# Latent attention of the second token stream in the first stream's PSUM banks: a hybrid attention, mLSTM and expert step on one core

## What is computed

```python
mod = (silu(cvec) @ ada_w[l] + ada_b[l])          # 1024 -> 6144, for both streams
sh1, sc1, g1, sh2, sc2, g2 = split(mod, 6)
xn = rms_norm(x, norm1_g[l]) * (1 + sc1) + sh1
aq, ak, av, bq, bk, bv, bo, bg, cq, ckv, ckr = split(xn @ w_in[l])   # 1024 -> 2096
oa = attention(norm(aq), norm(ak), av, sink)      # group A: 6 heads, 2 kv heads; stream 1 also sees 128 cached keys
ob = mlstm(bq, bk, bv, bo, bg, state)             # group B: 4 heads, both directions
oc = latent_attention(cq, ckv, ckr, w_uq, w_ukv)  # group C: 6 heads of 96; stream 1 also sees 128 cached tokens
x = x + g1 * (concat(oa, ob, oc) @ w_out[l])
x = x + g2 * ffn(rms_norm(x, norm2_g[l]) * (1 + sc2) + sh2)   # layer 0 dense SwiGLU, layer 1 top 2 of 8 experts
```

## Time and profile before

| | |
|---|---|
| median of 3 runs | 1622.07 us (1617.94 to 1623.02) |
| span of the profiled execution | 1619.0 us (the profile gives no other time of it) |
| TensorE busy | 1530.0 us, 95% |
| VectorE / ScalarE busy | 1164.3 us, 72% / 916.9 us, 57% |
| loads by the DMA | 523.26 MB, mean 323 GB/s |

### The profile page before, as it was taken

One profiled execution on the slowest core, in us unless ns is written; L12 is line 12 of the kernel. 1 busy time (PEld: TensorE's weight loads), 2 busy tenths in 40 slices (PEclk: granted clock), 3 DMA queues, 4 the chain that ended last, 5 costly groups with the idle time before them and its releaser, 6 DMA issues.

```text
span 1619.0 us, 19723 instructions
## 1 busy us (share of the span) xinstructions
PE 1530.0 (95%) x7058; PEld 1173.1 (72%) x7058; DVE 1164.3 (72%) x1222; ACT 916.9 (57%) x791; POOL 70.7 (4%) x113
## 2 busy tenths in 40 slices
PE   6888879999998788999999999999999999999998
PEld 3455448888656545788888888888888888888886
DVE  1364555444445355789888888888889888889998
ACT  1213234443232322677877877777877877777774
POOL 1610000000001000100000000000000000000200
PEclk9999999999997697899999999999999999999999
DMA  9969978865786275799999999999999999999994
GB/s 360 324 195 415 365 258 269 268 200 186 257 276 194 91 268 201 285 383 369 388 373 384 385 375 375 383 376 373 385 377 378 379 380 379 377 381 365 390 403 157
DMA packets 192825, 523.26 MB, mean 323 GB/s; under 512 B 10880, under 2 KB 71456, under 8 KB 187656
## 3 DMA queue, kind: packets, MB, share of 16 engines
q1 hardware_dynamic: 167440, 493.39, 82.7%
q0 software_dynamic: 7024, 18.63, 3.5%
q10 hardware_dynamic: 18312, 10.60, 2.2%
HBM read 505.50 MB, written 17.08 MB: 323 GB/s over the span
## 4 chain that ended last, share of the span: by engine, by line
PE 81%; DVE 9%; ACT 5%; issue 3%; DMA 3%; SPq 0%; DVEq 0%; ACTq 0%
PE PS L605 21%; PE PS L607 20%; PE PS L606 20%; PE PS L720 5%; PE PS L611 4%; DVE parts L2049 2%; PE PS L935 2%; DMA ring<-in_ada_w 2%; PE PS L686 1%; PE PS L734 1%; ACT parts L1442 1%; PE PS L750 1%; ACT arena L1279 1%; DMA ring<-in_w_in 1%; PE PS L625 1%
## 5 line engine op out<-in xcount | busy, mean ns | idle before, releaser
L2049 DVE TENSOR_TENSOR parts<-ring,parts 128x2048 fp32r<-128x2048 f32 x336 | 765.5, 2290 | 103.7 <-ACT parts L1442 101.1
L1442 ACT ACTIVATE parts<-ring 128x2048 fp32r<-128x2048 f32 x336 | 644.2, 1920 | 218.4 <-PE PS L607 218.4
L605 PE MATMUL PS<-parts 128*128 128x512 f32 x1608 | 634.4, 395 | 8.4 <-DVE parts L1688 4.1
L607 PE MATMUL PS<-parts 128*128 128x512 f32 x1608 | 627.9, 390 | 0.0
L606 PE MATMUL PS<-parts 128*128 128x512 f32 x1608 | 627.4, 390 | 0.0
L605 PEld LDWEIGHTS PS<-parts 128*128 128x128 f32 x1608 | 302.4, 188 | 76.5 <-DVE parts L2049 9.3
L607 PEld LDWEIGHTS PS<-parts 128*128 128x128 f32 x1608 | 302.3, 188 | 64.5
L606 PEld LDWEIGHTS PS<-parts 128*128 128x128 f32 x1608 | 302.6, 188 | 61.8 <-issue 0.2
L1602 DVE TENSOR_TENSOR parts<-ring,parts 128x2048 fp32r<-128x2048 f32 x33 | 75.5, 2289 | 52.4 <-PE PS L607 49.6
L720 PE MATMUL PS<-ring,xnT 128*128 128x420 f32 (+1 forms) x240 | 91.6, 532 | 0.0
L1220 ACT ACTIVATE parts<-ring 128x2048 fp32r<-128x2048 f32 x33 | 63.0, 1915 | 29.8 <-PE PS L607 29.8
(11 more groups left out here) (314 smaller groups left out, 939.4 us busy)
## 6 DMA issues: line engine op xcount, KB each, us to landing
ring<-in_moe_w SPq DMA_DIRECT2D x336, 1024.0 KB, 6.9
ring<-in_ada_w SPq DMA_DIRECT2D x40, 1024.0 KB, 9.6
ring<-in_w_in SPq DMA_DIRECT2D x32, 840.0 KB, 11.6
ring<-in_ffn_w SPq DMA_DIRECT2D x44, 512.0 KB, 5.4
ring<-in_w_out SPq DMA_DIRECT2D x16, 1024.0 KB, 8.0
ring<-in_ffn_w SPq DMA_DIRECT2D x11, 1024.0 KB, 4.8
expert_rows<-zeros ACTq DMA_DIRECT2D x17, 512.0 KB, 4.9
ring<-in_ada_w SPq DMA_DIRECT2D x16, 512.0 KB, 11.4
```

Of the source, the lines that this page charges most:

```text
L605: mm(out, s_hi, m_hi, start=start, stop=False)
L607: return mm(out, s_lo, m_hi, start=False, stop=stop)
L1442: A(w_hi(j), slot(n), ACT.Copy).then_inc(hi_ready, 1)
L2049: TT(w_lo(j, 3), slot(W0 + j), w_hi(j).bitcast(f32), ALU.subtract).then_inc(split_done, 1)
```

## The change

Stream 1's group C runs in banks 0 to 3 and in stream 0's scratch, that is in the places of C0 and not of A1 and B1. Its first step waits for C0's result (`oC`) and no longer for B1's (`num_read`). In turn stream 0's output projection (transposes in banks 4 and 5, result in 4 and 5) and the modulation pieces behind the first `A1` (banks 6 and 7) move to the banks in which B1 runs, and wait for B1's `num_read`. ScalarE's C1.3 has a new wait on the stores of the mLSTM's state, which lie in that scratch. The list is rewritten for both layers: C1's steps stand among A1's and B1's, and the `a` and `o0` tokens behind B1.5.

```diff
-PHASE_1 = {0: """
-A0 i1 A0 i1 A0 i1 A0 B0 i1 B0 i1 n1 B0 i1 i1 B0 B0 t0 i1 C0 t0 i1 C0 t0 i1 C0 a a a a a C0 g1 a C0 a a C0 a C0
-""", 1: """
-A0 i1 A0 i1 A0 i1 A0 B0 i1 B0 i1 n1 B0 i1 B0 B0 t0 i1 C0 t0 t0 i1 C0 i1 C0 i1 A1 A1 C0 g1 C0 l1 c1 A1 C0 A1 C0
-""}
-PHASE_2 = {0: """
-A1 l1 a A1 a c1 a a A1 a A1 B1 a B1 a B1 a o0 o0 B1 B1 a C1 t1 a C1 t1 t1 a C1 o0 a o0 a a C1 a C1 a a o0 C1 r0 r0 a C1
-""", 1: """
-a B1 a B1 a B1 o0 o0 B1 B1 a C1 t1 C1 t1 t1 a C1 o0 a o0 C1 a C1 a o0 C1 r0 r0 a C1
-""}
+ORDER = {0: """
+i1 A0 i1 A0 i1 A0 A0 B0 i1 B0 i1 n1 B0 i1 B0 i1 B0 t0 i1 C0 t0 i1 t0 C0 C0 i1 a a a C0 a a C0 g1 a a a C0 a
+c1 l1 A1 C0 A1 C1 C1 A1 C1 A1 B1 C1 B1 C1 B1 B1 C1 B1 a t1 t1 a t1 o0 a a C1 a o0 a o0 a o0 a a o0 r0 a a r0
+a a a a a a a
+""", 1: """
+A0 i1 A0 i1 i1 A0 i1 A0 B0 B0 n1 B0 B0 i1 B0 i1 t0 i1 C0 t0 t0 i1 g1 C0 i1 C0 i1 l1 A1 c1 C0 A1 C0 A1 C0 A1
+B1 C0 B1 C1 B1 B1 C1 B1 t1 C1 a a t1 a o0 a a a t1 a C1 o0 C1 o0 o0 C1 o0 r0 r0 a C1 a
+""}
...
+        def lane(X, s):
+            return 0 if X == "C" else s
...
         def oT(s):
-            return R(s, 4096 if s else QKT, 1024)
+            return R(1, 4096 if s else QK, 1024)
+
+        def o_banks(s):
+            return (6, 7) if s else (4, 5)
...
             l = 0 if g < early_of[0] else 1
-            return (4, 5) if g < g_after_1[l] else (2, 3)
+            return (4, 5) if g < g_after_1[l] else (6, 7)
...
                     if g == g_after_1[g >= early_of[0]]:
-                        wait("oC", 2 * (g >= early_of[0]) + 1)
+                        wait("num_read", 2 * (g >= early_of[0]) + 2)
...
             def group_C(l, s):
                 u = 2 * l + s
-                b0 = 4 * s
+                b0 = 0
                 wait("cn_ready", u + 1)
-                wait("num_read", u + 1)
                 if s == 0:
+                    wait("num_read", u + 1)
                     wait("state_copied", l + 1)
+                else:
+                    wait("oC", u)
...
             def out_proj(l, s):
                 wait("oC", 2 * l + s + 1)
+                if s == 0:
+                    wait("num_read", 2 * l + 2)
+                b0 = 0 if s else 4
...
                 if s == 1:
+                    act.wait_ge(state_out[l], 16 * 3)
                     summed(act, first["ukv", l, 1])
```

More of the change, by code:

```diff
@@ L31 @@
 PER_EXPERT = 3 * sum(PIECES)
-PHASE_1 = {0: """
-A0 i1 A0 i1 A0 i1 A0 B0 i1 B0 i1 n1 B0 i1 i1 B0 B0 t0 i1 C0 t0 i1 C0 t0 i1 C0 a a a a a C0 g1 a C0 a a C0 a C0
+ORDER = {0: """
+i1 A0 i1 A0 i1 A0 A0 B0 i1 B0 i1 n1 B0 i1 B0 i1 B0 t0 i1 C0 t0 i1 t0 C0 C0 i1 a a a C0 a a C0 g1 a a a C0 a
+c1 l1 A1 C0 A1 C1 C1 A1 C1 A1 B1 C1 B1 C1 B1 B1 C1 B1 a t1 t1 a t1 o0 a a C1 a o0 a o0 a o0 a a o0 r0 a a r0
+a a a a a a a
 """, 1: """
-A0 i1 A0 i1 A0 i1 A0 B0 i1 B0 i1 n1 B0 i1 B0 B0 t0 i1 C0 t0 t0 i1 C0 i1 C0 i1 A1 A1 C0 g1 C0 l1 c1 A1 C0 A1 C0
-"""}
-PHASE_2 = {0: """
-A1 l1 a A1 a c1 a a A1 a A1 B1 a B1 a B1 a o0 o0 B1 B1 a C1 t1 a C1 t1 t1 a C1 o0 a o0 a a C1 a C1 a a o0 C1 r0 r0 a C1
-""", 1: """
-a B1 a B1 a B1 o0 o0 B1 B1 a C1 t1 C1 t1 t1 a C1 o0 a o0 C1 a C1 a o0 C1 r0 r0 a C1
-"""}
-PLAN = [(PHASE_1[l] + PHASE_2[l]).split() for l in range(2)]
+A0 i1 A0 i1 i1 A0 i1 A0 B0 B0 n1 B0 B0 i1 B0 i1 t0 i1 C0 t0 t0 i1 g1 C0 i1 C0 i1 l1 A1 c1 C0 A1 C0 A1 C0 A1
+B1 C0 B1 C1 B1 B1 C1 B1 t1 C1 a a t1 a o0 a a a t1 a C1 o0 C1 o0 o0 C1 o0 r0 r0 a C1 a
+"""}
+PLAN = [ORDER[l].split() for l in range(2)]
 CONST = {}
@@ L727, in scores_softmax_out @@
                 u = 2 * l + s
-                b0 = 4 * s
+                sc = lane(X, s)
+                b0 = 4 * sc
                 for hi in range(6):
@@ L904, in group_C @@
                     wait("TC2_a", l + 1)
-                qkT = R(s, QKT, nh * 128, 96)
+                qkT = R(0, QKT, nh * 128, 96)
                 def qT(hi):
@@ L1287, in softmax @@
                 n = 512 * n_kt
-                A(R(s, QK, n), banks(4 * s, n), ACT.Copy).then_inc(Q["PT" + X + "_a"], 1)
+                A(R(sc, QK, n), banks(4 * sc, n), ACT.Copy).then_inc(Q["PT" + X + "_a"], 1)
                 yield
@@ L1340, in group_C @@
                     wait("C_mm", l + 1)
-                heads = R(s, QK, 18 * 96).rearrange("p (h d) -> p h d", h=18)
+                heads = R(0, QK, 18 * 96).rearrange("p (h d) -> p h d", h=18)
                 def halves(b, n):
                     return PS[:, b:b + 2, 0:n]
-                A(R(s, QK, 576).rearrange("p (a n) -> p a n", a=2), halves(b0, 288), ACT.Copy)
+                A(R(0, QK, 576).rearrange("p (a n) -> p a n", a=2), halves(b0, 288), ACT.Copy)
                 def kv(set_):
@@ L1718, in softmax @@
                 if X == "A":
-                    link(TT(c_(s, "ls"), c_(s, "ls"), c_(s, "es"), ALU.add))
-                link(v.reciprocal(c_(s, "rinv"), c_(s, "ls")))
+                    link(TT(c_(sc, "ls"), c_(sc, "ls"), c_(sc, "es"), ALU.add))
+                link(v.reciprocal(c_(sc, "rinv"), c_(sc, "ls")))
                 wait("PT" + X, u + 1)
                 n, all_ = 512 * n_kt, 768 * n_kt
-                v.tensor_copy(R(s, QK + n, all_ - n), banks(4 * s, all_)[:, n:all_]).then_inc(Q["PT" + X + "_d"], 1)
+                v.tensor_copy(R(sc, QK + n, all_ - n), banks(4 * sc, all_)[:, n:all_]).then_inc(Q["PT" + X + "_d"], 1)
                 yield
@@ L1899, in group_C @@
                 nh = 12 + 6 * s
-                qk = R(s, QK, nh * 96).rearrange("p (h d) -> p h d", h=nh)
-                sq = R(s, SQ, nh * 96).rearrange("p (h d) -> p h d", h=nh)
-                link(RED(c_(s, "tmp", nh), sq, AX.X, ALU.add))
-                link(TS(c_(s, "var", nh), c_(s, "tmp", nh), 1.0 / C_QK, EPS, ALU.mult, ALU.add))
-                r = rsqrt(s, nh)
+                qk = R(0, QK, nh * 96).rearrange("p (h d) -> p h d", h=nh)
+                sq = R(0, SQ, nh * 96).rearrange("p (h d) -> p h d", h=nh)
+                link(RED(c_(0, "tmp", nh), sq, AX.X, ALU.add))
+                link(TS(c_(0, "var", nh), c_(0, "tmp", nh), 1.0 / C_QK, EPS, ALU.mult, ALU.add))
+                r = rsqrt(0, nh)
                 last = TT(qk[:, 6:nh, :], qk[:, 6:nh, :], r[:, 6:nh].unsqueeze(2).broadcast_to([128, nh - 6, C_QK]), ALU.mult)
@@ L1911, in group_C @@
                     last = rope(tail, tail, K("cosC"), K("sinC"), 12, 16,
-                                [R(s, SQ + 192 * i, 192).rearrange("p (h d) -> p h d", h=12) for i in range(4)])
+                                [R(0, SQ + 192 * i, 192).rearrange("p (h d) -> p h d", h=12) for i in range(4)])
                 last.then_inc(Q["qkC_ready"], 1)
-                TS(c_(s, "sq"), r[:, 0:6], C_QK ** -0.5, None, ALU.mult)
+                TS(c_(0, "sq"), r[:, 0:6], C_QK ** -0.5, None, ALU.mult)
                 yield
```

65 lines of the change are left out of this document (33 added, 32 removed).

## The result

| | before | changed |
|---|---|---|
| median of 19 runs each | 1622.07 us (1617.91 to 1624.92) | 1626.17 us (1624.01 to 1632.16) |
| ratio | | 1.0034, interval 1.0024 to 1.0043 |
| span of the profiled execution | 1619.0 us | 1630.4 us (its run, 1631.97, is one of the slowest of the 19) |

Slower, as forecast, and inside the range; but 4.1 us and not 14. The profiled execution of the changed kernel lies 5.8 us above its median, so I compare stretches inside the two traces and leave the spans alone. A1.1 is the first step of stream 1's group A, B1.5 the last of its group B, and out1 the first transposes of its output projection behind the list; a stand is time in which TensorE is idle. First the stretches of the changed kernel, which answer to the earlier trace rows: length, busy us (instructions) of TensorE, its weight loads, VectorE, ScalarE and GpSimd, then TensorE clock, DMA share, GB/s.

The account below looks back on a forecast made before the run. The prediction took layer 0's mixer as bound by its loads and layer 1's by stream 1's chain A1, B1, C1. It summed 1622.07 + 20 (layer 0) - 5.6 (layer 1) = 1636 us, range 1625 to 1650.

Parts of the forecast that it names:

- +20: Layer 0: the FFN starts later because its loads arrive later, and nothing behind it gives this back; booked +20 us.
- -5.6: Layer 1: out1 starts 3.6 us earlier and 2 us come from the clock being up at its first products.
- bound of -14: Layer 1's best end: full clock from B1 on, about 8 us more gain than the booked -5.6.
- C1.1 and C1.2 come in with some 6 at half clock: Layer 1, way to B1.5: these two steps of C1, now ahead of it, add some 6 us.
- 4 and 9.6 us less: Layer 1, way to B1.5: two `a` pieces (4 us) and o0.2 with its stand (3.66 + 5.95) leave it.
- "faster" rival: Stream 1's two chains really run side by side: T 36 us after A1.1, layer 1 wins 14, 1613 us; 7%.
- T: Layer 0: the point at which a.10, the first `a` piece waiting for B1's read, may start; forecast 185.5 us.
- T to the FFN: Layer 0: loads and TensorE run side by side, the DMA's path is longer; FFN at T + 60.9, 246.4 us.
- the estimate from that ceiling: Layer 0: at 435 GB/s the 19.9 MB take 45.8 us, both paths are equal, and the layer loses 15.
- TensorE's path: Layer 0: by TensorE's own work and stands, out1 would start at T + 38.5 and the FFN at T + 54.8.
- the hole: Layer 0: a gap in the DMA's rate from about 155 to 186 us, the load ring being full until T.
- The much slower one: Rival: half clock in layer 0's whole stretch, T = 194.8, layer 0 +30 and layer 1 -2, 1650 us; 14%.

Follow-up runs that it names:

- the old head: Layer 0 as before, layer 1 as in the changed kernel, but layer 1's list up to the first A1 as before: 1605.91 us, again 1607.51 us.
- the new head: Layer 1 as in the changed kernel, with its rewritten list up to the first A1, layer 0 as before: 1602.32 us, again 1601.75 us.

## Why the prediction was right in sign and wrong in size

**The sum.** Forecast +20 and -5.6, together 14; measured +24.2 and -20.0, together 4. The way layer 0 loses and the sign of each layer were right. Layer 1's gain lay outside its own bound of -14, and the prediction had named a gain over 14 as what would make it wrong. That the time still fell inside the range, 1 us above its lower end, is luck: layer 0's loss, 4.2 us larger than booked, made up for a part of it.

**Layer 1, A1.1 to out1: the step that failed.** The prediction said "C1.1 and C1.2 come in with some 6 at half clock" and took the durations of a stretch with the clock at 0.62. Its sum is not clean here: 4 and 9.6 us less and 6 more put B1.5 38.7 us behind A1.1, its "about 5.6 earlier" 40.7. It came at 30.7, with the clock at 0.83, where it was 0.67 before. Two runs show which term was mis-sized. With C1 wholly behind B1 the way to B1.5 takes 32.7 us, and with C1.1 and C1.2 in it 30.2: the term booked at +6 measured -2.5, since the two steps run in stands of A1 and B1. And with the clock at 0.62 the same steps (the old head's first profile) took 40.0 us, about the forecast; at 0.83 and 0.84 they took 30.2 and 32.3. So the links were counted rightly, and the size was off by the clock and by the stands. The prediction carried over the granted clock of a stretch whose work the change itself rearranges. I had seen the bound ("full clock from B1 on, about 8 more") and put it at the end of the range and not in its middle. Up to C1.4 the forecast was 10.4 us too long (56.9 against 46.5), 8 to 10 of them ahead of B1.5. The rest of the 14.4 us is 1.3 from C1.4 to out1, 0.9 behind out1 (2.9 against 2), and 1.8 at the head, +3.0 against +4.8 by the distance from the FFN's first product (294.9 against 291.9).

**Where that gain came from.** C1 behind B1 leaves 5 us of the 20. The other 15 come from C1's first steps standing among A1's and B1's. For both together, the stands up to out1 fall from 20.9 in the kernel before to 11.0 us and the busy time from 73.2 to 63.0 us at an equal count of instructions (383 and 382). The prediction's "faster" rival had this mechanism for both layers; the Trainium skill, page "Perfetto Trace Analysis", section Optimization Strategy, says that interleaving regimes can gain. Layer 1 agrees with it, 20 us; layer 0 with the same interleaving lost 24.

**Layer 0, T.** Forecast A1.1 + 52.2, measured 53.5 (55.7, 53.0 and 55.9 in other profiles of this list). Right by its steps in the changed kernel's own profile: C1.3 to C1.4 took 12.63 us (forecast 12.6), B1.3 to B1.5 8.3 (8.5), the read 5.2 (4.7); C1.2 to C1.3 took 7.3 (5.25) and C1.4 to the scores 6.2 (4.5), both with pieces at half clock in them. The 3 us booked for the clock were a little short: the four profiles lie 3.7 to 6.6 us above the sum at full clock, 49.3. T came at 186.6 to 193.4 in the four profiles, inside the 182 to 195 named.

**Layer 0, T to the FFN.** Forecast 60.9, measured 63.5, and by nearly the steps given: the FFN's first load landed at T + 55.4 (forecast 52.7), and from the start of its split to the FFN's first product it took 8.1 (8.2). The 19.9 MB were reckoned at 389 GB/s, and the stretch from T to the FFN had 370. The Trainium skill, page "DMA: Bandwidth & Descriptors", section Bandwidth, puts the ceiling at 435 GB/s; the fastest 20 us behind T (210 to 230) had 422, but the whole way stayed well below, so the estimate from that ceiling, -15 for layer 0, was the worse one. TensorE's path, forecast at T + 54.8, was not refuted: the run with the a loads halved has 53.6 without its waits for loads. Relieving the loads alone gives back 6 of the 24 us. Two thirds of the loss lie ahead of T, as forecast; the lists that let B1 go ahead of C1.3, and `a` pieces into the hole, brought 12 and 16 of the 24 us back.

**Costed at nothing.** ScalarE's new wait for the state's stores cost nothing that a row shows: in C1.3 it waits 0.80 us, and for TensorE. That the head of layer 0's list shifts steps by under 0.5 us can't be told from the runs: A1.1 was forecast at 133.3 and came at 133.7, 134.1, 134.2 and 139.9 in four profiles of the list, so the scatter between executions is larger than the term.

**The rivals.** Of the faster one (7%), the gain of layer 1 came and exceeded its 14; its T at A1.1 + 36 did not. The much slower one (14%) is borne out in part: layer 0 from A1.1 to T had a clock of 0.75, below the 0.91 of before, and T lay at A1.1 + 53 to 56 instead of its 61. Of what was to show it, T, the `a` pieces' and the split's waits for loads came as named, and the hole too, from 165 to 195 instead of 155 to 186; the FFN came at 256.9 and not at 246; on the FFN's base C1.4 of layer 1 came 25.5 us earlier and not 13, and out1 17.1 and not 4; and layer 1 won more than 14, which the prediction had named as what would make it wrong.

**Best version.** Layer 1's change with layer 0 as before: 1602.3 and, again, 1601.75 us, 1.2 to 1.3% under before.

## What to carry to other kernels

Run each stage's part of a change alone before judging the whole: here a change that measured +0.3% was -1.2% in one layer and +1.5% in the other. Here the interleaving paid where the stage had stands to fill (layer 1, DMA share 0.59) and cost where the pieces that it pushed back were what kept the loads going (layer 0, DMA share 1.02). When a list is reordered, ask anew for TensorE's clock in the stretch: durations from a half-clock stretch hold only if its stands and its mix of products stay; and move a piece into a stand only after looking at what each of its operands waits for on the other engines.

## What the runs showed of the hardware

TensorE's granted clock in one stretch of one program is not fixed. The list with the old head ran A1.1 to B1.5 at 0.62 in one execution and at 0.84 in another, 40.0 and 32.3 us, and its eight times fall into 1603 to 1605 and 1608 to 1612. With the new head, whose wait at the start of the stretch is 1 us shorter (0.42 against 1.35 to 1.57), none of eight runs took over 1604; that the wait is the cause is not shown. It is so elsewhere too: in the same two executions out1 to the FFN in layer 0 took 16.3 us at 1.00 in the one and 19.2 us at 0.82 in the other. The first of these is the execution that had 0.62 in layer 1, so the two stretches do not fall together. The Trainium skill, page "TensorE: Matmul & The Clock Gate", section "What's actually happening", says that the same kernel shows different numbers of slow products from run to run; the two profiles of the old head agree that one program can differ. That note is about the start of a kernel, whose ramp it puts under 1% of a typical span; here the difference comes in the middle of the kernel and is 7.7 us of 1600 in one stretch, nearly twice what the whole change measured.
